# A transformer block with expert retrieval: 152 gathered tokens in three sets, dense expert products 360 wide

## The reference, cut to what matters

```python
q = (h @ w_peer_q).reshape(B, S, PEER_HEADS, 2, PEER_HALF)      # 8 heads, 2 halves of 128
s = einsum('bshcd,hckd->bshck', q, peer_keys)                   # 128 keys on each side
sv, si = lax.top_k(s, 16)                                       # 16 best of each side
cand = sv[..., 0, :, None] + sv[..., 1, None, :]                # 16 x 16 candidates
fv, fpos = lax.top_k(cand, 16)                                  # 16 experts of 128 x 128
g = softmax(fv)
# for each token t, its 8 heads h and its 16 experts k:
act = gelu(einsum('thkd,td->thk', peer_u[it], xt)) * gt
out = einsum('thk,thkd->td', act, peer_v[it])
```

## Time and profile before

| | |
|---|---|
| three runs | 3802.61 us median, 3800.97 to 3807.49 |
| profiled execution, its own time | 3803.27 us |
| its span | 3801.5 us |
| granted TensorE clock, mean | 0.997 |
| busy share TensorE / VectorE / ScalarE / GpSimd | 99% / 62% / 33% / 45% |
| moved by DMA | 800.91 MB |

### The profile page before, as it was taken

The page is one execution under the profiler, slowest core; times in us unless marked ns, Lnnn a source line. Parts: engine busy times, 40 slices in busy tenths (PEclk is TensorE's granted clock), DMA queues, the critical chain, the costliest instruction groups (busy, mean ns, idle before and its releaser), DMA issues.

```text
span 3801.5 us, 55133 instructions
## 1 busy us (share of the span) xinstructions
PE 3762.2 (99%) x20205; PEld 3452.8 (91%) x20205; DVE 2359.6 (62%) x4032; ACT 1263.2 (33%) x1639; POOL 1708.2 (45%) x1452
## 2 busy tenths in 40 slices
PE   8999999999999999999999999999999999999999
PEld 5778778888888887889999999999999999999999
DVE  5482453000000207886978888888888888888887
ACT  3433453333333323224642222222232222222222
POOL 1444334444444663444025555455544555654232
PEclk9999999999999999999999999999999999999999
DMA  6222112222222322224579899889888898889786
GB/s 208 89 89 100 67 67 88 99 99 90 98 99 99 134 99 104 106 105 153 218 281 340 322 339 332 316 320 331 327 290 296 318 338 312 319 315 335 278 292 216
DMA packets 187939, 800.91 MB, mean 211 GB/s; under 512 B 21024, under 2 KB 59944, under 8 KB 134440
## 3 DMA queue, kind: packets, MB, share of 16 engines
q1 hardware_dynamic: 100864, 492.61, 35.8%
q0 software_dynamic: 83840, 303.09, 22.3%
q10 hardware_dynamic: 3128, 3.88, 0.5%
HBM read 762.39 MB, written 37.09 MB: 210 GB/s over the span
## 4 chain that ended last, share of the span: by engine, by line
PE 94%; DMA 2%; DVE 2%; issue 1%; ACT 0%; POOL 0%; ACTq 0%; POOLq 0%; SPq 0%; DVEq 0%
PE bank L1816 94%; DMA grow<-v_rows,g_col 2%; DVE w_lo L1634 0%; DMA grow<-u_rows,g_col 0%; DVE g_acc L1669 0%; DMA tables<-wt 0%; PE bank L1985 0%; DVE xT L1688 0%; ACT w_hi L835 0%; POOL w_lo L766 0%; POOL grow L803 0%; DVE arena L1238 0%; PE bank L1992 0%; DVE arena L1247 0%; DVE smax L1364 0%
## 5 line engine op out<-in xcount | busy, mean ns | idle before, releaser
L675 POOL TENSOR_TENSOR p_lo<-ring,p_hi 128x512 fp32r<-128x512 f32 x432 | 563.5, 1305 | 669.3 <-ACT p_hi L835 669.3
L1816 PE MATMUL bank<-h_hi,w_hi 128*128 128x368 f32 (+1 forms) x2304 | 781.2, 339 | 10.2 <-DVE w_lo L1634 4.0
L1816 PE MATMUL bank<-h_lo,w_hi 128*128 128x368 f32 (+1 forms) x2304 | 775.4, 337 | 0.0
L1816 PE MATMUL bank<-h_hi,w_lo 128*128 128x368 f32 (+1 forms) x2304 | 775.2, 336 | 0.0
L1816 PE MATMUL bank<-act_hi,w_hi 128*128 128x368 f32 x2048 | 676.3, 330 | 0.5 <-DVE xT L1688 0.5
L1816 PE MATMUL bank<-act_hi,w_lo 128*128 128x368 f32 x2048 | 675.6, 330 | 0.0
L1816 PE MATMUL bank<-act_lo,w_hi 128*128 128x368 f32 x2048 | 671.1, 328 | 0.0
L835 ACT ACTIVATE w_hi<-ring 128x1024 fp32r<-128x1024 f32 (+1 forms) x351 | 408.6, 1168 | 680.4 <-PE bank L1816 653.5
L803 POOL DMA_INDIRECT grow<-v_rows,g_col x288 | 383.8, 1332 | 530.8 <-DVE g_acc L1669 358.3
L803 POOL DMA_INDIRECT grow<-u_rows,g_col x288 | 369.0, 1281 | 560.2 <-DVE grow L1662 243.8
L835 ACT ACTIVATE p_hi<-ring 128x512 fp32r<-128x512 f32 x464 | 292.7, 632 | 789.0 <-PE bank L1816 784.7
(11 more groups left out here) (224 smaller groups left out, 5410.0 us busy)
## 6 DMA issues: line engine op xcount, KB each, us to landing
ring<-w_exp SPq DMA_DIRECT2D x182, 1024.0 KB
ring_more<-w_exp SPq DMA_DIRECT2D x74, 1024.0 KB
ring<-w_mix SPq DMA_DIRECT2D x64, 1024.0 KB, 4.9
tables<-wt SPq DMA_DIRECT2D x12, 2048.0 KB, 6.5
wg<-tables SPq DMA_DIRECT2D x96, 256.0 KB
ring<-w_qk SPq DMA_DIRECT2D x20, 1024.0 KB, 4.9
ring<-w_o SPq DMA_DIRECT2D x16, 1024.0 KB, 4.9
ring<-w_pq SPq DMA_DIRECT2D x16, 1024.0 KB
```

Source lines behind the costliest of these rows:

```text
L675: nc.gpsimd.tensor_tensor(p_lo[:, part, :], ring[slot][:, part, :], p_hi[:, part, :].bitcast(F32), ALU.subtract).then_inc(quarter_lo, 1)
L1816: return nc.tensor.matmul(out, lhsT, rhs, start=start, stop=stop)
```

## The change

NX becomes 24, so ND is 360 and 152 tokens are gathered. The 24 further tokens go in two sets: set A of 16 tokens, put eight times over the partitions with 16 slots each, and set B of 8 tokens, put sixteen times with 8 slots each. That makes 128 + 16 + 8 = 152 rows of u and 152 of v. The number of rows of each step is now one list (`ROWS_AT`), u rows and v rows run through it in one order, with `FIRST_ROWS` giving 6, not 7, a full turn 23, and the turn from u to v 22 where it had 17. `LAST_ROWS` is as before; the tail has 28, not 26. Set A's rows come after the first 96, because `x_tok` must be filled again for set B. The tables lie in memory by group, not by block: a store writes 16 pieces of 1 KB from each partition where it wrote 16 KB in one, and a group's piece is read in 4 DMAs with runs of 3 KB, not 6 with runs of 1 KB.

```diff
-NX = 16
-NS = P // NX
+NX = 24
+NA, NB = 16, 8
+XA, XB = 16, 8
+XS = XA + XB
...
-ROWS_U = PAIRS + NX
-W_PIECES, G_PIECES = 6, 4
-TAIL_LESS = ((4, 6), (4, 6), (5,), (7,))
-MORE_DOT = (2, 5, 8, 10, 12, 14)
-MORE_ADD = (2, 5, 8, 10, 12, 14)
-FIRST_ROWS = (1, 2, 2, 1, 1)
+ROWS_U = PAIRS + XS
+U_HEAD = 96
+W_PIECES, G_PIECES = 4, 4
+FIRST_ROWS = (1, 1, 2, 1, 1)
...
-G_TURN, T_LAST, N_TURN = 6, 4, 12
+TURN_ROWS = (1, 1, 2, 1, 1, 2, 1, 1, 2, 1, 2, 2, 1, 2, 2, 1)
+MIDDLE_ROWS = (1, 2, 1, 2, 1, 1, 0, 1, 2, 1, 2, 2, 1, 2, 2, 1)
 LAST_ROWS = (1, 1, 2, 1, 1, 2, 1, 1, 2, 1, 2, 1, 0, 1, 0, 1)
+TAIL_ROWS = (1, 1, 1, 1, 0, 1, 1, 1) * 3 + (1,) * 7 + (0,)
+ROWS_AT = [N_FIRST]
+for n in (*TURN_ROWS * G_TURN, *MIDDLE_ROWS, *TURN_ROWS * (NG - LAG - G_TURN - 2), *LAST_ROWS, *TAIL_ROWS):
+    ROWS_AT.append(ROWS_AT[-1] + n)
...
-        table_dram = nc.dram_tensor("tables", [NTB, P, NKEYS * TB], F32).ap()
+        table_dram = nc.dram_tensor("tables", [NG, P, NTB * JG * TB], F32).ap()
...
-                sync.dma_start(table_dram[bass.ds(block, 1)].rearrange("a p n -> p (a n)"),
-                               wt[b][:, :, :].rearrange("p a b -> p (a b)")).then_inc(tab_out[b], 16)
+                part = slice(JG * TB * block, JG * TB * (block + 1))
+                sync.dma_start(table_dram[:, :, part].rearrange("g p n -> p g n"),
+                               wt[b][:, :, :].rearrange("p (g j) b -> p g (j b)", g=NG)).then_inc(tab_out[b], 16)
...
+            def spread_token(to, first, count):
+
+                pool.dma_start(x_tok[to:to + count, :, :], x_dram[first:first + count, :].rearrange("p (a n) -> p a n", a=KC)
+                               ).then_inc(x_spread, 16)
...
+            gather_all(0, half_rows[0], g_both, U_HEAD, x_both, begin=X_TURNS + P // NA)
+            gather_all(U_HEAD, half_rows[0], x_both, XA, g_both, at=U_HEAD)
+            rest, done = U_HEAD + XA, 0
+            for t in range((PAIRS - U_HEAD) // 4 - 1):
+                gather(rest, half_rows[0], g_both, t, U_HEAD)
+                if t == 1:
+                    pool.wait_ge(gath_free, 4 + 2 * rest)
+                for k in range(done, min(done + 3 if t else 0, P // NB)):
+                    spread_token(NB * k, NA, NB)
+                    done = k + 1
...
+            def gathered(tile):
+
+                if tile == T_LAST:
+                    turn_weights()
+                for i in range(ROWS_AT[tile], ROWS_AT[tile + 1]):
+                    if i < ROWS_U:
+                        a_u_row(i)
                     else:
-                        dot(N_DOT * g + m, m % 2)
...
+                        a_v_row(i - ROWS_U)
+                if tile == T_LAST - 1:
+                    turn_sums()
...
+                    if k == 0 and q == 0:
+                        v.memset(x_acc3, 0.0).then_inc(acc_zero, 1)
...
             for c in range(KC):
-                ins = mm(bank[4][:, NX * c:NX * c + NX], x_acc2[:, c, :], x_sel[:, :])
+                mm(bank[4][:, NX * c:NX * c + NA], x_acc2[:, c, :], x_sel[0])
+                ins = mm(bank[4][:, NX * c + NA:NX * c + NX], x_acc3[:, c, :], x_sel[1])
```

More of the change, by code:

```diff
@@ L1200, in _, with three_pairs @@
                         high_half(n % 2, half)
-            def three_pairs(t, first, turn=False):
+            def three_pairs(t, first, turn=None):
                 for q in range(6 * JG):
@@ L1582, in _ @@
             v.tensor_copy(x_wof[:, :], xw).then_inc(x_ready, 1)
-            v.reduce_sum(x_sel[:, :], ident[:, :].rearrange("p (s t) -> p t s", s=NS), AX_X).then_inc(x_ready, 1)
+            for sel, count in zip(x_sel, (NA, NB)):
+                v.reduce_sum(sel, ident[:, :].rearrange("p (s t) -> p t s", t=count), AX_X).then_inc(x_ready, 1)
             dve.wait_ge(tok_mm, 1)
@@ L1775, in _ @@
             assert done == N_FIRST
-            with dve.Fori(0, N_LOOP // 3) as t:
-                for r in range(3):
-                    experts(3 * t + r, r, dots)
-            for g in range(N_LOOP, G_TURN):
-                experts(g, g, dots)
-            experts(G_TURN, G_TURN, turn)
-            for g in range(G_TURN + 1, NG - LAG - 1):
-                experts(g, g, added)
-            experts(NG - LAG - 1, NG - LAG - 1, last_added)
-            added_rows = N_TURN + N_ADD * (NG - LAG - G_TURN - 2) + N_LAST
+            for g in range(NG - LAG):
+                experts(g, g, lambda g, q: gathered(2 * JG * g + q))
             for k in range(LAG):
@@ L1795, in _ @@
                         weigh_ahead(k + 1, q)
[L1796 to L1802 removed]
+                    gathered(n - R_V)
             dve.wait_ge(tail_tr, 1)
```

153 lines of the change are left out of this document (63 added, 90 removed).

## The result

The changed kernel takes **3815.98 us** (median of 14 runs, 3800.89 to 3823.08) beside 3802.73 us for the kernel before on the same chips (14 runs, 3798.55 to 3807.49). The ratio is 1.0031, 95% interval 1.0022 to 1.0040: slower by 13 us, where 3784 was forecast and 3812 was the end of the range. The profiled execution of the changed kernel took 3802.41 us (span 3800.6), so it is the second quickest of the 14; what it shows of waits is near the least that a run has, and a median run has 13.6 us more. One run of all that follow, in experiment 1, was in a slow state (4678 us); it is in no ratio and moves that median by 0.2 us.

What follows compares the result with a forecast made beforehand. TensorE's stream of matmuls (99% busy) was taken to bound the kernel; -39.1 - 1.7 - 4 + 3.5 + 2 + 17.7 + 3.4 = -18.2 us from 3803.3 gave 3785.1 profiled, 3784 us median; range 3758 to 3812.

Steps and rivals of the forecast that it cites:

- w: Main stage: growth of VectorE's waits for gathered rows per turn, taken as 4 us, bounds 0 to 7.
- Narrower products: Dense matmuls outside the table stage: 11712 of them gain 3.34 ns each from 8 fewer columns, -39.1 us.
- Table tile: Last table tile: one quarter block less, so 16 fewer TensorE records at 109 ns, -1.7 us.
- head: Between tables and main stage: one row instead of two, against a more scattered store, -4 us (bounds -6.0 to +5).
- The end: Behind the last product: `x_sel` has 32 matmuls for 16, 32 more records that nothing hides, +3.5 us.
- GpSimd: Turns 4 and 5: 16 `x_tok` DMAs where 8 stood delay the next gathers, +2 us (bounds 0 to 10).
- One row more a turn: Main stage: each turn needs 9.0 us of spare time; turns 8, 9 and 10 lack it, +17.7 us of TensorE waits.
- clock: Main stage: two TensorE waits for `w_lo` drop the granted clock, +3.4 us (none to five: 0 to 8.5).
- A: Main stage and head: nothing new is waited for and rows land in time, 3759 us; chance 0.24.
- B: Turns 7 to 10: gather loop is full in v turns at 5.76 us a row, 3796 us; chance 0.16.
- C: Half turns: traffic ceiling of 359 GB/s adds 3.0 us in ten turns, 3791 us; chance 0.06.
- D: Ten full turns: gather loop decides everywhere at 5.76 us a row; slower, 3841 us; chance 0.10.

Runs made afterwards that it cites:

- experiment 1: Tables laid out by expert group alone in the kernel before: 3809.34 us; the changed kernel with tables by block as before: 3825.11 us.
- experiment 2: The kernel before with dense products 360 wide, still 144 gathered tokens and 22 rows a turn: 3782.03 us.
- quickest version: Changed kernel, first row of a two-row step used between VectorE's low halves, 11 and 12 rows per half turn, single spreading transfers: 3774.29 us (transfers in threes: 3774.83).
- pairs apart: Changed kernel, first row of a step with two rows used between VectorE's two low halves, not behind both: 3782.68 us.
- even order: Changed kernel with 11 and 12 rows in a turn's halves, not 10 and 13, and no neighbouring two-row steps: 3819.57 us alone.
- experiment 5: Changed kernel, separately: weight loads as two 512 KB transfers, 3816.37 us; 11 and 12 rows per half turn, 3819.57 us; `x_tok` transfers one at a time, 3811.81 us.
- Experiments 6 and 7: Changed kernel: activation cast moved from VectorE to ScalarE, 3816.83 us; separately, first row of two-row steps used between VectorE's low halves, 3782.68 us.
- both edits of 5: 11 and 12 rows per half turn, and `x_tok` transfers one at a time; each alone in the changed kernel: 3819.57 and 3811.81 us.

## Why the prediction was wrong

In the profiled execution the sum was 3785.1 us and 3802.4 came, 17.3 us more; the median run adds 13.6 more over it. Two steps failed. The gain of the products was 11.8 us too large, because two widths were taken to fix the time of a third. And the price of the row was too small, because waits for rows were put in as one even w that a turn's sum of spare time can pay, where they came in lumps and the spare time stood in other steps. Term by term:

- **Narrower products, -39.1.** Mis-sized. The step that failed is the straight line: two widths fixed the slope, and 360 was taken to lie on it. Over long stretches it doesn't, by 1.0 ns. 11712 x 2.33 ns = 27.3 us, so 11.8 us of the forecast gain never were there. Two points always lie on a line, so their fit was no support, and no rival and no part of the range had another slope. Long stretches show 164.4 ns and some shorter ones 160.0 (experiment 2); which of them a width gets was not in the rows of the kernel before.
- **Table tile, -1.7, and head, -4.** The first step of the main stage came at 1987.5, 6.0 us earlier, where 8.9 were forecast. 1.0 us of that is the narrower products again. The waits that should have gone with the row stayed, 2.4 and 2.0 us beside 2.2 and 2.1; only the fall of the clock behind them went. So the head gave about 2 us, and the row taken from there did not shorten the waits. Whether the store alone holds them was not tried.

```profile
PE bank L1813 <- DVE w_lo L1657: 2.4, 1, 2.4
PE bank L1813 <- DVE w_lo L1613: 2.0, 1, 2.0
```

- **The end, +3.5.** From the last product to the end of the span it is 16.6 us, before 10.7. The 32 more records cost the 3.5 us as said. About 2 us more come from the clock: the 64 records last from 3783.97 to 3793.06, 9.1 us, where 64 x 109 ns are 7.0, and the clock falls at 3788.8, in the middle of them and not, as before, behind the 32 (3795.2). The window of the end of the changed kernel shows it:

```profile
3784.00:3801.00 17.00, 12.71 (x81) 12.31 (x79) 4.26 (x7) 0.00 (x0) 0.00 (x0) 0.64 0.37 118
```

- **GpSimd, +2.** Mis-sized. Turn 5, where set B is spread, is 10.3 us over 126.2, the size of the upper bound. It is 127.1 without set B, and 126.2 in the quickest versions with all its transfers (three in a row in one of them). So the transfers cost nothing with the pairs apart and the even order, and 5 to 14 us without one or both; one fixed sum was the wrong form.
- **One row more a turn, w = 4, +17.7, and clock, +3.4.** The mechanism was right: longer waits for rows make `w_lo` late and TensorE waits. As an average w was nearly right in the profiled execution: the waits for rows grew by 56 us in twelve turns, 4.7 each. It is one of the quickest, though; three profiles of variants of experiment 5, of 3810 to 3822 us, have 193 to 207 us of such waits, which makes w 6 to 7, the end of the bounds. The twelve turns together lost 29.6 us against 126.2 each (19 in waits of TensorE, the rest its lower clock), where 23 were forecast beside the 5 of turns 10 and 11 that the kernel before had already. But "turns 0 to 5 have it" was wrong: they lost 16.5 us of it. It failed in two ways. First, w was not even: against the kernel before, the waits for rows grew by 7.9, 9.9 and 17.5 us in turns 1, 2 and 5 and by 2.5 at most in turns 0, 3 and 4. For turn 5 the transfers are a cause; why turns 1 and 2 and not 3 and 4 stays open. Second, the step treated spare time as a purse that a turn can draw on anywhere, and turns 1 and 5 lost time with 5.0 and 2.8 us of it left. VectorE waits for ScalarE in some steps and for rows in others, and the buffers let it be only about a tile ahead. Experiments 6 and 7 fit that: work taken off in steps 0 to 7 bought nothing, waits taken off in the pairs bought 33 us.
- **The run-to-run part.** No term covered that this kernel spreads: 3801 to 3823 us in 14 runs, where the quickest version spreads from 3770 to 3775 in four. No median run of the changed kernel was profiled. But in the seven profiles with 23 rows and the old placement (this one, and those of experiments 1, 5 and 6) the profiled times run from 3802.4 to 3825.0 us and the twelve turns from 1544.1 to 1565.8, so nearly all of the difference between such runs is time lost in the twelve turns: the kernel with the even order alone took 3822.0 us, with 1561.2 us of turns and 32 us of TensorE's waits. The further 13.6 us of the median are most likely the same.
- **The bounds.** "Its own range, 3767 to 3798" has a low end with every bound in it, but its high end has w = 7 alone. With the other upper bounds that the text names (the head +5, GpSimd +10, five falls of the clock) and the same sum of four turns it is 3820, which includes the 3816 that came.

**Rivals.** A (nothing waited for, 3759) could not come: even half the bytes gave 3770, since the products alone gain less. B had the right scale for the quickest runs, but not only v turns lose: turns 1, 2 and 5 lost 16 us, turns 7 to 11 13. C falls: the waits went without a byte less, and the quickest version (pairs apart, both edits of 5) moves more than C's 359 GB/s in the second half of turn 8, with TensorE busy throughout. Its windows of turn 8 and of that half:

```profile
2994.80:3121.00 126.20, 126.20 (x770) 126.20 (x769) 113.89 (x129) 36.74 (x40) 74.45 (x73) 1.00 0.94 350
3058.00:3121.00 63.00, 63.00 (x386) 63.00 (x385) 57.22 (x60) 17.26 (x17) 39.81 (x38) 1.00 0.96 368
```

The Trainium skill, page "DMA: Bandwidth & Descriptors", section Specifications, has about 358 GB/s as the limit of a core, half of the 716 GB/s of a stack that two cores share. With one core at work the trace goes above it, 368 GB/s over 63 us, so here it is no limit; over this whole turn 350 was asked for. D is the side that came, at 13 us and not at 38: its argument, "a late row delays `w_lo` at once", is what the timeline shows, and so is its sign, u turns over 127 us (turns 1, 2 and 5); its rate of 5.76 us a row in every turn is not. The chance of 0.13 for slower was too small, in part because the gain that slower had to eat up was 11.8 us too large: against 29.5 us of gain left, D's point of decision lies at 3.0 us a turn, not 4.1.

## What to carry to other kernels

Read spare time by its place, not by its sum: when one in-order engine both feeds TensorE and waits for transfers, look at what stands behind each wait, and put needed work between two uses of the same transfer ring before taking any work away. When the width of a matmul is changed by little, take its time from a run at that width, since two other widths don't fix it to a nanosecond, and thousands of matmuls multiply it. Try the order of the work together with the change: the change lost 13 us in one order, and 28 us were gained with another, 6 of which the kernel before gains too. And before two chains are compared, look how far back each was followed, and before two profiles are, where each stands among the runs of its kernel.

## What the runs showed of the hardware

- Matmuls of 360 columns start 164.4 ns apart over long stretches, those of 368 and 512 columns 166.7 and 226.7 ns: 8 columns less save 2.3 ns where the straight line gives 3.3. But in some stretches of the same kernel, at the same granted clock, 360 columns start 160.0 ns apart (289 matmuls in 46 us, where 281 is the rule).
- One core alone moved 368 GB/s over 63 us, with the DMA engines busy 0.96.
- A gather of 512 KB lands 6.6 to 6.9 us behind its issue (medians) with the DMA engines busy 0.89 to 0.95, and halving the rows of the weight loads beside it made that 7.2 to 7.3, not less.
- The granted clock fell at waits of TensorE of 1.8 to 3.1 us, for 3.4 or 6.8 us, and did not fall at one of 3.3 us.
- Small fp32 matmuls of 16 and 8 columns, 112 ns apart without a gap, did not keep the granted clock up: it fell to 1.2 GHz 4.7 us after the last wide product, while they were still running.
